# Expert routing in a two-block transformer kernel: logits, softmax and token selection put in another order, and one small row of sums computed at another place

## The reference, cut to what matters

```python
x = x + g1[:, None, :] * out_l
h_l = modulate(rmsnorm(x, norm2[l]), sh2, sc2)
x = x + g2[:, None, :] * ec_moe(h_l, w_router[l], w_e_gate[l], w_e_up[l], w_e_down[l])

def ec_moe(x, w_router, w_e_gate, w_e_up, w_e_down):
    B, T, D = x.shape
    cap = CAP_FACTOR * T // N_EXPERTS          # 32
    aff = jax.nn.softmax((x @ w_router).astype(jnp.float32), axis=-1)
    g, idx = lax.top_k(aff.transpose(0, 2, 1), cap)
    xs = jax.vmap(lambda xb, ib: xb[ib])(x, idx)
    a = jnp.einsum('becd,edf->becf', xs, w_e_gate)
    u = jnp.einsum('becd,edf->becf', xs, w_e_up)
    y = jnp.einsum('becf,efd->becd', jax.nn.silu(a) * u, w_e_down) * g[..., None].astype(x.dtype)
    return jax.vmap(lambda yb, ib: jnp.zeros((T, D), x.dtype).at[ib.reshape(-1)].add(yb.reshape(-1, D)))(y, idx)
```

## Time and profile before

| | |
|---|---|
| median of 3 runs | 2181.14 us (2177.85 to 2185.31) |
| the profiled execution's own time | 2176.91 us |
| its span, first to last instruction | 2175.1 us |
| TensorE busy | 1915.3 us (88%) |
| VectorE, ScalarE busy | 771.7 us (35%), 524.1 us (24%) |
| bytes moved | 414.13 MB, 190 GB/s over the span |
| mean granted TensorE clock | 0.941 |
| chain that ended last | PE 60%, DMA 20%, DVE 12%, ACT 7% |

### The profile page before, as it was taken

The page is one execution under the profiler, slowest core; times in us unless marked ns, Lnnn a source line. Parts: engine busy times, 40 slices in busy tenths (PEclk is TensorE's granted clock), DMA queues, the critical chain, the costliest instruction groups (busy, mean ns, idle before and its releaser), DMA issues.

```text
span 2175.1 us, 26152 instructions
## 1 busy us (share of the span) xinstructions
PE 1915.3 (88%) x11290; PEld 1442.1 (66%) x11290; DVE 771.7 (35%) x1306; ACT 524.1 (24%) x784; POOL 0.2 (0%) x4
## 2 busy tenths in 40 slices
PE   7999999999998999998999999998999876565654
PEld 6799876799997898766799998546888421111111
DVE  3442332655533533234355665323544200000001
ACT  2201121244432011211344463423442210000000
POOL 0000000000000000000000000000000000000000
PEclk9999999999999999999999999999999897677778
DMA  6222342465532223453745442211127799999997
GB/s 249 97 97 87 127 155 97 155 193 186 183 117 97 97 97 116 155 194 136 240 155 174 158 129 64 97 39 39 40 78 306 304 409 409 409 409 409 409 409 291
DMA packets 170323, 414.13 MB, mean 190 GB/s; under 512 B 4832, under 2 KB 61408, under 8 KB 166752
## 3 DMA queue, kind: packets, MB, share of 16 engines
q1 hardware_dynamic: 169488, 408.69, 50.8%
q10 hardware_dynamic: 720, 3.78, 0.4%
HBM read 411.41 MB, written 1.05 MB: 190 GB/s over the span
## 4 chain that ended last, share of the span: by engine, by line
PE 60%; DMA 20%; DVE 12%; ACT 7%; issue 1%; SPq 0%; ACTq 0%; DVEq 0%
PE ps L219 44%; PE ps L767 7%; DMA ring<-in_w_e_down_dram 5%; ACT rarena L213 5%; DMA high<-in_w_e_up_dram 5%; DVE rarena L178 4%; PE ps L1157 3%; PE ps L1514 2%; DVE low L178 2%; DMA ring<-in_w_e_up_dram 2%; DMA high<-in_w_e_down_dram 2%; DMA high<-in_w_e_gate_dram 2%; DMA ring<-in_w_e_gate_dram 2%; DVE high L178 2%; ACT high L213 1%
## 5 line engine op out<-in xcount | busy, mean ns | idle before, releaser
L219 PE MATMUL ps<-high,ring 128*128 128x256 f32 (+1 forms) x2016 | 482.7, 391 | 7.5 <-DMA ring<-in_w_in_dram 5.6
L219 PE MATMUL ps<-rarena 128*128 128x256 f32 (+1 forms) x3648 | 460.0, 288 | 9.6 <-DVE rarena L178 7.4
L219 PEld LDWEIGHTS ps<-rarena 128*128 128x128 f32 x3648 | 448.3, 192 | 19.6 <-DVE rarena L178 10.4
L219 PEld LDWEIGHTS ps<-high,ring 128*128 128x128 f32 x2016 | 376.4, 192 | 81.4 <-issue 20.2
L213 ACT ACTIVATE high<-ps 128x512 f32<-128x512 f32 (+2 forms) x210 | 103.3, 492 | 719.0 <-PE ps L1514 286.8
L1514 PE MATMUL ps<-high,low 128*32 128x512 f32 x1040 | 168.2, 780 | 103.0 <-DMA high<-in_w_e_up_dram 36.4
L178 DVE TENSOR_TENSOR rarena<-ring,rarena 128x2048 fp32r<-128x2048 f32 x76 | 167.3, 2201 | 137.5 <-ACT rarena L213 135.8
L1514 PEld LDWEIGHTS ps<-high,low 128*32 128x32 f32 x1040 | 32.1, 129 | 224.0 <-issue 62.0
L213 ACT ACTIVATE rarena<-ring 128x2048 fp32r<-128x2048 f32 x76 | 140.0, 1841 | 157.0 <-DMA ring<-in_w_ffn_up_dram 92.7
L178 DVE TENSOR_TENSOR high<-high,ps 128x512 f32<-128x512 f32 x52 | 35.7, 687 | 324.8 <-PE ps L1514 267.0
L219 PE MATMUL ps<-low,ring 128*128 128x256 f32 (+1 forms) x544 | 128.0, 392 | 14.9 <-DVE low L192 5.5
(11 more groups left out here) (149 smaller groups left out, 1364.9 us busy)
## 6 DMA issues: line engine op xcount, KB each, us to landing
ring<-in_w_in_dram SPq DMA_DIRECT2D x34, 2048.0 KB, 7.9
high<-in_w_e_gate_dram SPq DMA_DIRECT2D x22, 2048.0 KB, 24.0
high<-in_w_e_up_dram SPq DMA_DIRECT2D x22, 2048.0 KB, 24.1
high<-in_w_e_down_dram SPq DMA_DIRECT2D x21, 2048.0 KB, 24.0
ring<-in_w_mod_dram SPq DMA_DIRECT2D x12, 2048.0 KB, 8.7
ring<-in_w_ffn_gate_dram SPq DMA_DIRECT2D x22, 1024.0 KB, 5.4
ring<-in_w_ffn_up_dram SPq DMA_DIRECT2D x22, 1024.0 KB, 8.0
ring<-in_w_e_down_dram SPq DMA_DIRECT2D x11, 2048.0 KB, 24.3
```

Source lines behind the costliest of these rows:

```text
L219: ins = self.e.matmul(out, l, r, start=first and i == 0, stop=end and i == n - 1)
```

## The change

It has six parts. crow is computed behind the four QK steps of gates2 instead of ahead of attention, in an "m" bank, and VectorE copies it between the first eight BD matrices and the other sixteen. The logits' matmuls of chunks 2i and 2i+1 stand behind output tile 4+i. VectorE adds the eight squares up as they are made, and one pair of matmuls with ones takes the place of eight, with one square root for both halves. The softmax subtracts the maximum in one operation on both halves, takes one exponential without a sum, and sums, inverts and multiplies on VectorE. The transposes of aff stand ahead of those of h2. The first comparison for Sm is one operation on both halves instead of two.

```diff
@@ tensor_program
-            b = take_bank(7, "crow.ps", "crow")
-            PE.group(b[:, 0:16], [(mod[:, 24 + i, 0:1].to_broadcast([128, 128]), wrt[:, i, :])
-                                  for i in range(8)]).then_inc(*PE("crow.ps"))
             fill = [gates2()]
             mix([heads_of(q) for q in range(3)] + [stats()], fill, AT_PLAN, False)
             PE.mark("attended.pe")
             pool["p"] = [6, 7]
             mix([iter(range(QK_STEPS))], fill, [1], False)
+            b = take("m", "crow.ps", "crow")
+            PE.group(b[:, 0:16], [(mod[:, 24 + i, 0:1].to_broadcast([128, 128]), wrt[:, i, :])
+                                  for i in range(8)]).then_inc(*PE("crow.ps"))
...
-            for i in range(4):
-                b = take_bank(4 + i % 2, f"tx{4 + i}.ps", f"x2{4 + i}")
-                PE.group(b[:, 0:256], [(w[:, k, 128 * i:128 * i + 128], T.yT[:, k, :]) for k in range(8)]).then_inc(
-                    *PE(f"tx{4 + i}.ps"))
-            PE.mark("to1.used")
-            pool["m"], pool["p"] = [0, 1, 2, 3, 4], [5, 6, 7]
-
-
-            bs = [take_bank(t, f"tok.ss{t}", f"tok.sqrt{t}") for t in range(2)]
             bl = [take_bank(6 + t, f"lgt{t}.ps", f"logits{t}") for t in range(2)]
-            for i in range(8):
-                PE.wait_ge(f"z{i}.x", f"sq{i}.x")
-                for t in range(2):
-                    ins = PE.e.matmul(bs[t][:, 0:1], E.sq[:, i, 128 * t:128 * t + 128], ones[:, 0:1], start=i == 0,
-                                      stop=i == 7)
-                    if i == 7:
-                        ins.then_inc(*PE(f"tok.ss{t}"))
+
+            def logits_of(i):
+
+                PE.wait_ge(f"z{i}.x")
                 for t in range(2):
                     ins = PE.e.matmul(bl[t][:, 0:16], E.h2[:, i, 128 * t:128 * t + 128], wrt[:, i, :], start=i == 0,
                                       stop=i == 7)
                     if i == 7:
                         ins.then_inc(*PE(f"lgt{t}.ps"))
+
+            for i in range(4):
+                b = take_bank(4 + i % 2, f"tx{4 + i}.ps", f"x2{4 + i}")
+                PE.group(b[:, 0:256], [(w[:, k, 128 * i:128 * i + 128], T.yT[:, k, :]) for k in range(8)]).then_inc(
+                    *PE(f"tx{4 + i}.ps"))
+                if i == 3:
+                    PE.mark("to1.used")
+                logits_of(2 * i)
+                logits_of(2 * i + 1)
+            pool["m"], pool["p"] = [0, 1, 2, 3, 4], [5, 6, 7]
+
+
+            b = take_bank(0, "tok.ss", "tok.sqrt")
+            PE.wait_ge("sq7.x")
+            for t in range(2):
+                ins = one(b[:, t:t + 1], E.sq[:, 0, 128 * t:128 * t + 128], ones[:, 0:1])
+            ins.then_inc(*PE("tok.ss"))
+            PE.wait_ge("aff")
+            b = take_bank(7, "at.ps", "at")
+            transposes([(b[0:16, 128 * t:128 * t + 128], E.aff[:, t, :]) for t in range(2)]).then_inc(*PE("at.ps"))
             for t in (1, 0):
                 for hh in range(2):
...
-            PE.wait_ge("aff")
-            b = take_bank(7, "at.ps", "at")
-            transposes([(b[0:16, 128 * t:128 * t + 128], E.aff[:, t, :]) for t in range(2)]).then_inc(*PE("at.ps"))
@@ scalar_program
-            for t in range(2):
-                A.wait_ge(f"tok.ss{t}")
-                A.act(E.rsc[:, t:t + 1], ps(f"tok.ss{t}")[:, 0:1], ACT.Sqrt, scale=1.0 / 1024, bias=misc(1)).then_inc(
-                    *A(f"tok.sqrt{t}"))
+            A.wait_ge("tok.ss")
+            A.act(E.rsc, ps("tok.ss")[:, 0:2], ACT.Sqrt, scale=1.0 / 1024, bias=misc(1)).then_inc(*A("tok.sqrt"))
             A.e.preload_act_table(Exp)
             A.wait_ge("lmax")
-            for t in range(2):
-                A.act(E.aff[:, t, :], E.lg[:, t, :], Exp, bias=E.rs[:, t, 1:2], accum=E.rs[:, t, 2:3]).then_inc(
-                    *A(f"aff{t}"))
+            A.act(E.aff, E.lg, Exp).then_inc(*A("exps"))
@@ vector_program
-            V.wait_ge("crow.ps")
-            V.cp(crow, ps("crow.ps")[:, 0:16]).then_inc(*V("crow"))
...
                           c("bd").rearrange("p (n k) -> p n k", k=4), mul, mul).then_inc(*V(f"bd{z}{i}"))
+                if z == 0:
+                    V.wait_ge("crow.ps")
+                    V.cp(crow, ps("crow.ps")[:, 0:16]).then_inc(*V("crow"))
...
-                    V.tt(E.sq[:, i, :], x[:, i, :], x[:, i, :], mul).then_inc(*V(f"sq{i}.x"))
-            V.wait_ge("tok.sqrt1")
+                    V.tt(E.sq[:, i, :], x[:, i, :], x[:, i, :], mul).then_inc(*V())
+                    if i:
+                        V.tt(E.sq[:, 0, :], E.sq[:, 0, :], E.sq[:, i, :], add).then_inc(*V(f"sq{i}.x"))
+            V.wait_ge("tok.sqrt")
...
-            V.ts(E.rs[:, :, 1], E.rs[:, :, 0], -1.0, mul).then_inc(*V("lmax"))
-            V.wait_ge("aff1")
+            each = lambda z: z.unsqueeze(2).to_broadcast([128, 2, 16])
+            V.tt(E.lg, E.lg, each(E.rs[:, :, 0]), sub).then_inc(*V("lmax"))
+            V.wait_ge("exps")
+            V.reduce(E.rs[:, :, 2], E.aff, add).then_inc(*V())
             V.recip(E.rs[:, :, 0], E.rs[:, :, 2]).then_inc(*V())
-            for t in range(2):
-                V.ts(E.aff[:, t, :], E.aff[:, t, :], E.rs[:, t, 0:1], mul).then_inc(*V())
+            V.tt(E.aff, E.aff, each(E.rs[:, :, 0]), mul).then_inc(*V())
...
-            for t in range(2):
-                V.ts(E.Sm[:, t, 0:128], ps("bx.ps")[:, 0:128], misc(4 + t), ALU.is_equal).then_inc(*V())
+            V.tt(E.Sm[:, :, 0:128], ps("bx.ps")[:, 0:128].unsqueeze(1).to_broadcast([128, 2, 128]),
+                 c("misc")[:, 4:6].unsqueeze(2).to_broadcast([128, 2, 128]), ALU.is_equal).then_inc(*V())
```

## The result

| | before | changed |
|---|---|---|
| median, us (12 runs each) | 2180.72 (2177.85 to 2188.09) | 2175.90 (2170.57 to 2179.41) |
| ratio of the two | | 0.9973 [0.9961, 0.9986] |
| the profiled execution's time, us | 2176.91 | 2178.25 |
| its span, us | 2175.1 | 2176.4 |
| mean granted clock | 0.941 | 0.956 |

The table holds a contradiction that the rest of this text is about: the two medians say 4.8 us faster, the two profiled executions 1.3 us slower. The sum of the prediction was +1.7 for the profiled pair.

What follows compares the result with a forecast made beforehand. The time was taken as set by when the first gate weights are used up (1708.3 us), with TensorE's chain before and weight transfers after. +6.5 and -4.8 gave +1.7: 2178.6 profiled, 2182.9 on the median, range 2177 to 2188.

Steps and rivals of the forecast that it cites:

- Crow, the place it leaves: Ahead of attention: without crow's 16 records the first scores start earlier, gain 0.86 us (bounds 0 and 1.71).
- Crow, the place it goes to: Among BD's products: VectorE waits for crow, 6.2 us later (5.5 to 6.5), plus 1.2 us of lower clock (0 to 1.8).
- Logits between the last output tiles: End of the output tiles: tile 7 comes 2.7 us later, but the last square root is done 3.2 us earlier.
- Rival (d): Logits steps behind each tile wait for ScalarE, eating 3 of the routing's 4.8 us: 2186 us; chance 0.05.
- Softmax, turn, comparison: Routing: shorter softmax gains 0.6 us, aff's transposes ahead of the tokens 0.4, one comparison for two 0.3.
- The clock at the first weights: From first tokens to freed buffer: shorter wait by the sixteen transposes, gain 0.3 us (bounds 0 and 2.7).
- Rival (b): Transposes or the shorter stop hold the clock up at the first weights: 2.3 us more gain, 2180.6; chance 0.12.
- rival (c): Routing is earlier but the expert weight stream is not, so the 4.8 us is lost: 2187.7 us; chance 0.07.
- Rival (a): The wait for crow at BD is hidden by cover behind VectorE: -5.7 us, 2175.4; chance 0.08.
- The sum: Whole kernel: +6.5 ahead of the border, -4.8 at it, net +1.7 us: 2178.6 profiled, 2182.9 on the median.

Runs made afterwards that it cites:

- the 20 executions: All profiled executions together, of the kernel before, the changed kernel and the follow-up kernels; attention took some 114 us in 4 of 9 with crow ahead of it.
- crow elsewhere: Profiled executions of kernels that compute crow behind attention or in TensorE's idle ahead of the output projection; none of eleven had attention of some 114 us.
- the crow kernel: The kernel before with crow alone moved behind the QK steps of gates2, nothing else: 2184.87 us, ratio 1.0012 to the kernel before.
- the routing alone: The changed kernel with crow back ahead of attention, everything at the routing as changed: 2176.36 us, ratio 0.9978 to the kernel before.
- crow in the gap: The changed kernel with crow computed in TensorE's 2.28 us idle ahead of the output projection: 2169.50 us, ratio 0.9956 to the kernel before.

## Why the prediction was right or wrong

**Crow, the place it leaves.** -0.76 instead of -0.86: the scores' last releaser was a memset of VectorE, a little later than the copy by which I had set their start. Right.

**Crow, the place it goes to.** 6.02 us of VectorE's wait, 4.59 of TensorE's idling, releasers as named. Right. The clock behind it was taken at 1.2 of 0 to 1.8; about 1.5.

**Logits between the last output tiles.** Tile 7 is 2.68 later (2.7), its root ends 2.4 us behind it (2.4); with the 8.25 of the kernel before that is -3.1 to the -3.2. Only the last step waits for its scaled tile, 0.77 us, and a step behind a tile costs what was said. Rival (d) is refuted.

**Softmax, turn, comparison.** From the exponential to the finished weights 0.87 us (0.94), from there to MAX8 0.69 instead of 1.17 (-0.5 to -0.4), the comparison 0.42 for 0.78 (-0.36 to -0.3). Right.

**The clock at the first weights** was too small: I took 0.3 of 0 to 2.7, and it was 1.3. The spreading pair runs at 1.00, and VectorE waits 0.58 instead of 0.89 for it; the first gates finish 0.99 us sooner. Three stretches of the changed kernel:

```profile
1699.00:1702.50 3.50, 3.50 (x18) 3.38 (x16) 2.89 (x11) 1.91 (x3) 0.00 (x0) 0.50 1.01 405
1703.00:1706.00 3.00, 0.48 (x2) 0.29 (x2) 2.25 (x9) 0.50 (x1) 0.00 (x0) 1.00 0.73 289
1706.50:1709.50 3.00, 3.00 (x16) 2.10 (x20) 1.07 (x2) 0.73 (x2) 0.00 (x0) 0.50 0.01 3
```

The eighteen transposes run at 0.50, the clock then rises while TensorE stands, and falls again for the gather and the first weights. Rival (b) came true in part: 1.0 of its extra 2.3.

The rule of the Trainium skill that the prediction weighed (TensorE: Matmul & The Clock Gate, Part 4: PE-mode transpose) would have left this term at 0. The trace disagrees once more, with nothing but transposes ahead of the 1.00 (eighteen from 1698.77 on, behind 2.6 us without work).

The last row also refutes rival (c): the transfers still run dry ahead of the tenth load, 3 GB/s, and 5.9 us earlier at the border is 5.9 us earlier for the stream. Rival (a), with its wait hidden, lies nearest to the median measured and is refuted all the same: the wait stands in every execution of the changed kernel.

**The sum** is right for the executions it was made on: +1.7 forecast, +1.3 found. Its own terms measured +1.0. The rest is luck, since the unchanged stretch up to 1384 and a longer spell of lower clock in attention added 1.7 and the last stretch took 1.4, 1.3 of it because the kernel before met a lower clock behind its last transfer. The unchanged stretch alone takes 1379.7 to 1386.9 us in the 20 executions, so a single pair can agree or disagree with a sum by that much.

**The step that failed** is the sentence "the same sum on the median gives 2182.9". It took the 4.2 us by which the median lay above the profiled execution for a constant that the change keeps. They were no constant. 47 runs of the kernel before in the first two measurements average some 2181.6, and its slow stretches are matters of the single execution: up to 8.9 us in attention, up to 2.9 in the logits loop, up to 2.9 at the end. The profiled execution had the first not at all, and of the others 0 and 1.3. The new loop ends the second, and none of eleven executions with crow elsewhere has the first or the third.

As an estimate from the profiles, the kernel before loses on average 3.9 us in attention (4 of the 9 executions with crow ahead, some 8.9 us each), 0.9 in the loop (two of its four, 2.86 less the 1.0 that comes back) and 1.8 at the end (its four against 14.5), 6.6 in all. From the +1.0 of the terms that makes -5.6; measured by the means: -5.8 and -3.4. The same estimate takes the crow kernel from +7.0 to +1.3 (measured +2.2), the routing alone from -5.9 to -6.8 (measured -5.9), and crow in the gap from -6.7 to -13.3 (measured -11.6). So it is good to about 2 us. What is shown is where the time lies and that the new loop ends one of the three spells; that crow's place ends the other two is argued from counts, and why the clock falls in one execution and not in another stays open.

## What to carry to other kernels

A profiled execution is one draw: before a forecast rests on it, set its time beside the runs' average, and where they differ by more than the effect, take a second and a third profile and compare them stage by stage. A change that takes away a place where the clock can fall, such as a loop of thin matmuls, can be worth more than its own trace shows. A small product is best put where its engine stands anyway: crow cost 0.8 us ahead of attention, 7.7 behind it and nothing that could be seen in a gap of 2.28 us, and all three places differed by one move in the program.

## What the runs showed of the hardware that was not expected

- TensorE's granted clock can be 0.50 for 15 us and more while TensorE is busy without a break. It began behind sixteen 4x4 matmuls (1.94 us) and went on through score matmuls of 512 columns, some of them on 64 partitions; the stage was 8.9 us longer. In 16 of 20 executions the stage took 105.4 to 106.3 us instead.
- One-column and 16-column matmuls lose the clock at a moment that varies: four of them with one column took 0.58 us at 1693.34 and 0.99 at 1694.39, in the same loop; in the profiled execution of the kernel before the same step comes 4.8 us after the loop's start.
- Behind the last transfer the same sixteen matmuls took 1.92 us at a granted clock of 1.00 and 3.24 at 0.50, and from that landing to the end one kernel took 14.5 to 17.4 us.
- The exponential started 0.06 us after the 1.28 us of its table load (1696.50 + 1.28 to 1697.84); no other cost of the load is to be seen.
